# Split-weight slots shifted by 128 bytes each, and odd projection tiles streamed backwards

## The chip, the cores and the metric

The kernel runs on one core of one Trainium2 chip. Its time is the device time of that core in microseconds. It stood at 1546.92 us, the median of two executions (1546.09 and 1547.75 us).

## The reference

Two transformer blocks, one after the other, on 512 tokens of width 1024, all in float32. The first block: a mixer of spatial gating and a gated delta rule, cross-attention to a memory of 256 tokens, a feed-forward of width 4096 with squared relu. The second: a mixer of a causal convolution and sliding-window attention with rotary positions, and a gated feed-forward of width 2816. Nearly all of the arithmetic is in projections, products of the 512 tokens with a weight matrix, between norms:

```
proj = h @ w_in                                  # 1024 x 4104
return jnp.concatenate([y_a, y_b], axis=-1) @ w_out
q = (h @ w_q) ; k = (m @ w_k) ; v = (m @ w_v) ; o @ w_o
return jnp.square(jax.nn.relu(h @ w1)) @ w2      # 1024 x 4096, 4096 x 1024
proj = u @ w_in[l] + b_in[l]                     # 1024 x 5888
up, gate = jnp.split(u @ w_ffn_up[l], 2, axis=-1)
x = x + (jax.nn.silu(a) * gate) @ w_ffn_down[l]
```

## The kernel before

**Layout.** Activations lie transposed: 128 channels on the partitions, the 512 tokens along the free dimension, eight such tiles for the width of 1024. A projection is cut into output tiles of 128 channels. `WEIGHTS` (`weight_order`, line 73) lists 274 of them in the order in which they are multiplied, each as (name, n, k0, k1): output tile n of the matrix called name, over the input tiles k0 to k1, mostly eight.

**Split products.** A float32 product is made of three products in float32r: operands are split into a high part (rounded to float32r by a copy on ScalarE) and a low part (the rest, subtracted on VectorE). For every input tile k, TensorE multiplies high by high, high by low and low by high into the same PSUM bank (lines 1239, 1240 and 1241). The weights are the stationary operand (128x128), the activations the moving one (128x512). So an output tile of eight input tiles is 24 matmuls, each with a load of its own of the stationary operand. The moving operand is in a_hi and a_lo (normed inputs) or b_hi and b_lo (results that are projected again).

**Slots.** Weights come by DMA into w_raw, four slots of 128x1024 (`SLOTS`, 4096 bytes per partition each), tile j in slot j % 4. ScalarE writes w_hi (step `split`, line 1535), VectorE w_lo (step `low`, line 1818), each with four slots too; `split_weights` (line 850) names the place of tile j. The split of tile j waits until tile j - 4 is multiplied. The load into w_raw of tile j waits for both splits of tile j - 4. The eight tiles that come last are kept from an earlier use (`KEPT`), four of them in a_hi and a_lo. The first three tiles are loaded and split together, input tile by input tile (step `front`).

**Order.** `SCHEDULE`, written partly by hand, is one list of steps that all engines go through; each step of an engine waits on semaphores for its operands. Projection steps (`mm`) use banks 0 to 3, tile j bank j % 4; the work between (norms, the delta rule, attention, transposes, all in plain float32) uses banks 4 to 7. Tile j waits until tile j - 4 has been read out of its bank, which VectorE does in most cases.

**Widths.** The moving operand has 512 columns save in the projection of the memory's keys (xa_wk, 256), in the last output tiles (`HALVES`: down2a and down2b, 256 tokens each) and in xa_wv, where the roles are turned (lines 1207 to 1209).

**Places in a partition.** The buffers lie one after the other in the order of their declarations, each start rounded up to 32 bytes. w_raw, w_hi, w_lo, a_hi and a_lo are whole multiples of 512 bytes and begin at the same place of a 512-byte line; line_pad (96 bytes) brings the region of xs, b_hi and b_lo to that place too. Every 128x128 block of the stationary operand is 512 bytes per partition, so it begins at that place as well.

Of the kernel before, what the change touches and what calls it, by code (L numbers as in the profile page):

```python
# [9 lines left out]
F32R = mybir.dt.float32r  # L10
# [5 lines left out]
P = 128  # L16
D = 1024
KT = D // P
S = 512
# [19 lines left out]
SLOTS = 4  # L39
# [4 lines left out]
STRIP = 32  # L44
# [695 lines left out]
def chunk(c):  # L740
    return slice(c * P, (c + 1) * P)


def build_program(nc, x_in, mem_in, front_in, logits_in, weights_in, ws_in, columns_in, rows_in, sinks_in, matrices_in,
                  positions_in, out):
    with ExitStack() as base:
        def sbuf(name, shape, dtype=F32, stack=None):
            return (stack or base).enter_context(nc.sbuf_tensor(name, shape, dtype))
# [9 lines left out]

        raw = sbuf("w_raw", [P, SLOTS, KT * P])
        raw_front = raw[:, 0:FRONT, :].rearrange("p j c -> p (j c)").rearrange("p (t c) -> p t c", t=KT)  # L760
        w_hi = sbuf("w_hi", [P, SLOTS, KT * P], F32R)
        w_lo = sbuf("w_lo", [P, SLOTS, KT * P], F32R)
        a_hi = sbuf("a_hi", [P, KT, S], F32R)
        a_lo = sbuf("a_lo", [P, KT, S], F32R)
        columns = sbuf("columns", [P, N_COLUMNS])
# [83 lines left out]

        def split_weights(j):  # L850
            if j < FIRST_EXTRA:
                return w_hi[:, j % SLOTS, :], w_lo[:, j % SLOTS, :]
            at = (j - FIRST_EXTRA) * 2
            return tuple(a[:, at:at + 2, :].rearrange("p t s -> p (t s)") for a in (a_hi, a_lo))

# [301 lines left out]
        def tensor_program(pe):  # L1157
# [22 lines left out]
            for kind, n in SCHEDULE:  # L1180
# [11 lines left out]
                elif kind == "mm" and WEIGHTS[n[0]][0] == "xa_wv":  # L1192
                    j = n[0]
# [7 lines left out]
                    for i in range(2):  # L1201
                        k, at = first + i, slice(i * S, (i + 1) * S)
                        q.wait_ge(*stage_act.at((A_MEMORY, k)))
                        q.wait_ge(*stage_dve.at((A_MEMORY, k)))
                        for c in range(MC):
                            to = value_bank(half, c)
                            pe.matmul(to, m_hi[:, k, chunk(c)], w_hi[:, j % SLOTS, at], start=k == 0, stop=False)  # L1207
                            pe.matmul(to, m_hi[:, k, chunk(c)], w_lo[:, j % SLOTS, at], start=False, stop=False)  # L1208
                            t = pe.matmul(to, m_lo[:, k, chunk(c)], w_hi[:, j % SLOTS, at], start=False, stop=k == KT - 1)  # L1209
                    t.then_inc(mm_pe.handle, 1)  # L1210
                elif kind == "mm":
                    j, ka, kb = n
                    name, i, k0, k1 = WEIGHTS[j]
                    tokens = HALVES[name][1] if name in HALVES else slice(0, S)
                    width = M if name in ("xa_wk", "xa_wv") else tokens.stop - tokens.start
                    to, loaded = banks[j % BANKS][:, 0:width], j if j < N_LOADS else j - KEPT
                    weights_hi, weights_lo = split_weights(loaded)
# [8 lines left out]
                    for k in range(ka, kb):  # L1226
                        if name in OPERAND:
                            g = OPERAND[name]
                            hi, lo = (m_hi[:, k, :], m_lo[:, k, :]) if g == A_MEMORY else (a_hi[:, k, :], a_lo[:, k, :])
                            q.wait_ge(*stage_act.at((g, k)))  # L1230
                            q.wait_ge(*stage_dve.at((g, k)))
                        else:
                            g = b_generation(name, k0)
                            t = k - k0
                            hi, lo = b_hi[:, b_slot(g, t), tokens], b_lo[:, b_slot(g, t), tokens]
                            q.wait_ge(*b_act.at((g, t)))
                            q.wait_ge(*b_dve.at((g, t)))
                        at = slice((k - k0) * P, (k - k0 + 1) * P)
                        pe.matmul(to, weights_hi[:, at], hi, start=k == k0, stop=False)  # L1239
                        pe.matmul(to, weights_hi[:, at], lo, start=False, stop=False)  # L1240
                        t = pe.matmul(to, weights_lo[:, at], hi, start=False, stop=k == k1 - 1)  # L1241
# [8 lines left out]
                elif kind == "root" and n == A_LAST:  # L1250
                    to = side("sum", n)
# [5 lines left out]
                    for c in range(MC):  # L1257
                        t = pe.matmul(to[:, c:c + 1], square("square", (n, KT - 1))[:, chunk(c)], ones[:, 0:1], start=False, stop=c == MC - 1)
# [11 lines left out]
                elif kind == "row":  # L1270
                    width = M if n in (A_MEMORY, *HALF_OF) else S
# [6 lines left out]
                elif kind == "logits":  # L1278
# [4 lines left out]
                    for k in range(KT // STRIPS):  # L1283
                        for c in range(STRIPS):
                            at = c * (KT // STRIPS) + k
                            t = pe.matmul(side("logits")[strip(c), :], logits_w[:, at, :], x0[:, at, :], start=k == 0, stop=k == KT // STRIPS - 1)
                    t.then_inc(logits_pe.handle, 1)
                elif kind == "rates" and n == 0:
# [4 lines left out]
                    for c in range(NC):  # L1293
                        t = pe.matmul(logits[:, c, :], temp("logits")[:, chunk(c)], half_matrix(SUM_STRIPS)[:, 0:2 * H], start=True, stop=True)
# [12 lines left out]
                elif kind == "sums":  # L1307
# [3 lines left out]
                    for c in range(NC):  # L1311
                        t = pe.transpose(side("sums", n)[:, chunk(c)], qkv[:, n, chunk(c)], eye)
                    t.then_inc(sums_pe.handle, 1)
                elif kind == "statistics":
# [3 lines left out]
                    for c in range(NC):  # L1318
                        t = pe.transpose(bank[:, chunk(c)], temp("v", n)[:, chunk(c)], eye)
                    t.then_inc(statistics_pe.handle, 1)  # L1320
                elif kind == "mix":
# [4 lines left out]
                    for c in range(NC):  # L1326
                        t = pe.matmul(bank[:, chunk(c)], temp("normed", n)[:, chunk(c)], ws[:, n, :], start=True, stop=True)
# [6 lines left out]
                elif kind == "strict":  # L1334
# [6 lines left out]
                    for c in range(NC):  # L1341
                        pe.matmul(kk_bank[:, chunk(c)], kh[:, c, :], kh[:, c, :], start=True, stop=True)
                        t = pe.matmul(qk_bank[:, chunk(c)], kh[:, c, :], qh[:, c, :], start=True, stop=True)
                    t.then_inc(strict_pe.handle, 1)
                elif kind == "turn":
# [3 lines left out]
                    for c in range(NC):  # L1349
                        for part in BLOCKS:  # L1350
                            t = pe.matmul(blocked(bank)[part, c, :], inv_tb[n % 2][part, c, :], half_matrix(EYE_BLOCKS)[part, :],
                                          start=True, stop=True)
                    t.then_inc(turn_pe.handle, 1)
                elif kind == "level_y":
# [10 lines left out]
                    for c in range(NC):  # L1365
                        if level < LEVELS - 1:
                            for part in BLOCKS:
                                t = pe.matmul(blocked(bank)[part, c, :], b[part, c, :], x[part, c, :], start=True, stop=True)  # L1368
                        else:
                            t = pe.matmul(blocked(bank)[BLOCKS[1], c, :], strict_t[h % 2][BLOCKS[0], c, BLOCKS[1]], x[BLOCKS[0], c, :],  # L1370
                                          start=True, stop=True)
# [1090 lines left out]
```

## Time and profile before

| | |
|---|---|
| Two executions | 1546.09 us, 1547.75 us; median 1546.92 us |
| Profiled execution, first to last instruction (span) | 1544.6 us |
| TensorE busy | 1534.5 us, 99% of the span, 8150 matmuls |
| Weight loads busy | 1270.0 us, 82% |
| VectorE, ScalarE, GpSimd busy | 875.9 us (57%), 605.9 us (39%), 103.5 us (7%) |
| Read from HBM | 143.29 MB, 94 GB/s over the span |

The page has no time of the profiled execution beside its span. A busy time is the union of an engine's instructions; matmuls overlap in the records, so the busy times of groups of matmuls add up to more than the span, and the mean duration of one is longer than the distance to the next. The distance between two starts is read from the instructions in order of time. The chain of waits follows the work back from the last instruction. Idle time of VectorE or ScalarE costs nothing as long as TensorE is not waiting for them.

### The profile page before, as it was taken

How to read it: one execution, taken by the hardware profiler on the slowest of the kernel's cores; microseconds unless marked ns; L12 is line 12 of the kernel's file. 1: busy time of each engine (PE TensorE's matmuls, PEld its weight loads, DVE VectorE, ACT ScalarE, POOL GpSimd, SP SyncE). 2: the span in 40 equal slices, each digit the busy share in tenths (PEclk: the TensorE clock that was granted, in tenths of full speed). 3: DMA queues.
4: the chain of work that ended last, by engine and by line, in shares of the span. 5: the costliest groups of instructions: out<-in, count | busy, mean ns of one | idle time of the engine just before them, and what ended most of it. 6: DMA issues, size and time to landing. Idle time of an engine off the chain costs nothing.

```text
span 1544.6 us, 20434 instructions
## 1 busy us (share of the span) xinstructions
PE 1534.5 (99%) x8150; PEld 1270.0 (82%) x8150; DVE 875.9 (57%) x1336; ACT 605.9 (39%) x979; POOL 103.5 (7%) x87
## 2 busy tenths in 40 slices
PE   9999999999999999999999999999999999999998
PEld 7888889887788888888888887877888888888887
DVE  7777766654454343436556777543555653664565
ACT  6546334533343241323556343533244331332333
POOL 0000202110020000000140000100011000000000
PEclk9999999999999999999999999999999999999999
DMA  7121213521133223222322232222332232222212
GB/s 269 56 69 35 77 69 125 189 82 57 57 106 109 94 86 107 95 97 89 108 96 68 84 114 91 94 77 69 116 104 87 99 107 96 92 99 98 93 63 74
DMA packets 44861, 146.70 MB, mean 95 GB/s; under 512 B 4960, under 2 KB 8288, under 8 KB 44640
## 3 DMA queue, kind: packets, MB, share of 16 engines
q1 hardware_dynamic: 42592, 141.93, 27.3%
q10 hardware_dynamic: 2176, 3.47, 0.7%
q8 instruction: 65, 1.06, 0.3%
q14 instruction: 28, 0.23, 0.0%
HBM read 143.29 MB, written 2.10 MB: 94 GB/s over the span
## 4 chain that ended last, share of the span: by engine, by line
PE 98%; issue 1%; DVE 0%; DMA 0%; ACT 0%; POOLq 0%; POOL 0%; DVEq 0%; SPq 0%; ACTq 0%
PE bank L1239 29%; PE bank L1241 29%; PE bank L1240 29%; PE bank L1457 1%; PE bank L1474 1%; PE bank L1368 1%; PE bank L1396 1%; PE bank L1401 1%; PE bank L1491 0%; PE bank L1207 0%; PE bank L1209 0%; PE bank L1208 0%; PE bank L1514 0%; PE bank L1503 0%; PE bank L1169 0%
## 5 line engine op out<-in xcount | busy, mean ns | idle before, releaser
L1239 PE MATMUL bank<-a_hi,w_hi 128*128 128x512 f32 (+1 forms) x1275 | 497.2, 390 | 0.0
L1241 PE MATMUL bank<-a_hi,w_lo 128*128 128x512 f32 (+1 forms) x1275 | 490.0, 384 | 0.0
L1240 PE MATMUL bank<-a_lo,w_hi 128*128 128x512 f32 (+1 forms) x1275 | 489.6, 384 | 0.0
L1818 DVE TENSOR_TENSOR w_lo<-w_raw,w_hi 128x1024 fp32r<-128x1024 f32 (+2 forms) x259 | 327.3, 1268 | 146.6 <-ACT w_hi L1535 146.2
L1535 ACT ACTIVATE w_hi<-w_raw 128x1024 fp32r<-128x1024 f32 (+2 forms) x259 | 266.2, 1034 | 206.8 <-PE bank L1241 198.2
L1239 PEld LDWEIGHTS bank<-a_hi,w_hi 128*128 128x128 f32 x1275 | 239.6, 188 | 49.3 <-issue 2.4
L1241 PEld LDWEIGHTS bank<-a_hi,w_lo 128*128 128x128 f32 x1275 | 239.5, 188 | 48.0
L1240 PEld LDWEIGHTS bank<-a_lo,w_hi 128*128 128x128 f32 x1275 | 239.7, 188 | 45.8 <-issue 0.2
L1239 PE MATMUL bank<-b_hi,w_hi 128*128 128x512 f32 (+1 forms) x720 | 276.5, 384 | 0.0
L1240 PE MATMUL bank<-b_lo,w_hi 128*128 128x512 f32 (+1 forms) x720 | 275.1, 382 | 0.0
L1241 PE MATMUL bank<-b_hi,w_lo 128*128 128x512 f32 (+1 forms) x720 | 275.1, 382 | 0.0
L1239 PEld LDWEIGHTS bank<-b_hi,w_hi 128*128 128x128 f32 x720 | 135.3, 188 | 26.8 <-issue 0.9
L1240 PEld LDWEIGHTS bank<-b_lo,w_hi 128*128 128x128 f32 x720 | 135.4, 188 | 26.3 <-issue 0.2
L1241 PEld LDWEIGHTS bank<-b_hi,w_lo 128*128 128x128 f32 x720 | 135.3, 188 | 26.3
L2102 DVE TENSOR_TENSOR xs<-xs,bank 128x512 f32<-128x512 f32 (+1 forms) x88 | 55.9, 636 | 127.9 <-PE bank L1241 120.8
L1802 DVE TENSOR_TENSOR temp<-bank,rstd 128x512 f32<-128x512 f32 x101 | 69.3, 687 | 64.0 <-PE bank L1241 59.4
L1810 DVE SCALAR_TENSOR_TENSOR temp<-temp,columns 128x512 f32<-128x512 f32 x96 | 72.2, 752 | 28.6 <-ACT temp L1774 17.2
L2290 POOL TENSOR_TENSOR square_sum<-square_sum,square 128x512 f32<-128x512 f32 x28 | 39.8, 1422 | 616.4 <-ACT square L1570 616.4
L2080 DVE TENSOR_TENSOR b_lo<-temp,b_hi 128x512 fp32r<-128x512 f32 x62 | 42.9, 692 | 59.3 <-ACT b_hi L1676 59.0
L1676 ACT ACTIVATE b_hi<-temp 128x512 fp32r<-128x512 f32 x62 | 39.2, 633 | 84.0 <-DVE temp L2259 58.3
L1717 ACT ACTIVATE temp<-temp 128x512 f32<-128x512 f32 x32 | 20.2, 632 | 93.2 <-DVE temp L2155 93.2
L2281 POOL TENSOR_TENSOR narrow<-narrow,columns 128x4 f32<-128x4 f32 (+1 forms) x13 | 19.4, 1494 | 412.1 <-DVE narrow L1861 375.3
(319 smaller groups left out, 1198.3 us busy)
## 6 DMA issues: line engine op xcount, KB each, us to landing
w_raw<-weights_in SPq DMA_DIRECT2D x247, 512.0 KB, 3.2
w_raw<-weights_in SPq DMA_DIRECT2D x8, 384.0 KB, 2.9
x_first<-x_in SPq DMA_DIRECT2D x8, 256.0 KB, 5.9
xs<-x_in ACTq DMA_DIRECT2D x2, 1024.0 KB, 10.8
w_raw<-weights_in SPq DMA_DIRECT2D x8, 256.0 KB, 2.7
mem_x<-mem_in SPq DMA_DIRECT2D x1, 1024.0 KB, 7.8
out<-xs SPq DMA_DIRECT2D x8, 128.0 KB, 1.8
w_raw<-front_in SPq DMA_DIRECT2D x5, 192.0 KB, 5.9
```

What stands on the lines that cost most here:

```text
L1239: pe.matmul(to, weights_hi[:, at], hi, start=k == k0, stop=False)
L1240: pe.matmul(to, weights_hi[:, at], lo, start=False, stop=False)
L1241: t = pe.matmul(to, weights_lo[:, at], hi, start=False, stop=k == k1 - 1)
L1535: act.activation(split_weights(n)[0][:, 0:size], raw[:, n % SLOTS, 0:size], ACT.Copy).then_inc(split_act.handle, 1)
L1676: act.activation(b_hi[:, b_slot(g, i), :], x, ACT.Copy).then_inc(b_act.handle, 1)
L1717: act.activation(temp("relu", n), temp("relu", n), ACT.Square).then_inc(relu_act.handle, 1)
L1802: return dve.tensor_tensor(to, full(name, n, k0)[0:to.shape[0], 0:width], scale[0:to.shape[0], 0:width], ALU.mult)
L1810: dve.scalar_tensor_tensor(acc, buf[:, at:at + S], weight(i), acc, ALU.mult, ALU.add).then_inc(done.handle, 1)
L1818: dve.tensor_tensor(lo[:, 0:size], raw[:, n % SLOTS, 0:size], hi[:, 0:size].bitcast(F32), ALU.subtract).then_inc(split_dve.handle, 1)
L2080: dve.tensor_tensor(lo, x, hi.bitcast(F32), ALU.subtract).then_inc(b_dve.handle, 1)
L2102: dve.tensor_tensor(xs[:, t, tokens], xs[:, t, tokens], full(name, t, k0)[:, 0:tokens.stop - tokens.start], ALU.add).then_inc(residual_dve ...
L2290: pool.tensor_tensor(total, total, square("square", n)[:, 0:total.shape[1]], ALU.add).then_inc(square_pool.handle, 1)
```

## The change

w_hi and w_lo get 32 more elements (`STRIP`, 128 bytes) per slot, which no instruction reads or writes; slot s then begins s x 128 bytes further in a 512-byte line than slot 0. Everything behind the two buffers moves by 2 x 4 x 128 = 1024 bytes. In the projection steps, an output tile with odd n (here i) and a moving operand of 512 columns reads that operand from the last token to the first, and writes its bank from the last column to the first, in all three matmuls of each input tile; the bank then holds what it held before. Tiles with even n, those of 256 columns, xa_wv and the first three tiles (n = 0, 4 and 8 of qkv) run forward.

```diff
--- before.py
+++ after.py
@@ -758,8 +758,8 @@
 
         raw = sbuf("w_raw", [P, SLOTS, KT * P])
         raw_front = raw[:, 0:FRONT, :].rearrange("p j c -> p (j c)").rearrange("p (t c) -> p t c", t=KT)
-        w_hi = sbuf("w_hi", [P, SLOTS, KT * P], F32R)
-        w_lo = sbuf("w_lo", [P, SLOTS, KT * P], F32R)
+        w_hi = sbuf("w_hi", [P, SLOTS, KT * P + STRIP], F32R)
+        w_lo = sbuf("w_lo", [P, SLOTS, KT * P + STRIP], F32R)
         a_hi = sbuf("a_hi", [P, KT, S], F32R)
         a_lo = sbuf("a_lo", [P, KT, S], F32R)
         columns = sbuf("columns", [P, N_COLUMNS])
@@ -849,7 +849,7 @@
 
         def split_weights(j):
             if j < FIRST_EXTRA:
-                return w_hi[:, j % SLOTS, :], w_lo[:, j % SLOTS, :]
+                return w_hi[:, j % SLOTS, 0:KT * P], w_lo[:, j % SLOTS, 0:KT * P]
             at = (j - FIRST_EXTRA) * 2
             return tuple(a[:, at:at + 2, :].rearrange("p t s -> p (t s)") for a in (a_hi, a_lo))
 
@@ -1236,6 +1236,11 @@
                             q.wait_ge(*b_act.at((g, t)))
                             q.wait_ge(*b_dve.at((g, t)))
                         at = slice((k - k0) * P, (k - k0 + 1) * P)
+                        if i % 2 and width == S:
+                            pe.matmul(to[:, ::-1], weights_hi[:, at], hi[:, ::-1], start=k == k0, stop=False)
+                            pe.matmul(to[:, ::-1], weights_hi[:, at], lo[:, ::-1], start=False, stop=False)
+                            t = pe.matmul(to[:, ::-1], weights_lo[:, at], hi[:, ::-1], start=False, stop=k == k1 - 1)
+                            continue
                         pe.matmul(to, weights_hi[:, at], hi, start=k == k0, stop=False)
                         pe.matmul(to, weights_hi[:, at], lo, start=False, stop=False)
                         t = pe.matmul(to, weights_lo[:, at], hi, start=False, stop=k == k1 - 1)
```

## Rows read from the trace of the kernel before

**Rows 1.** The page: span, busy time by engine, granted clock by slice.

```profile
span 1544.6 us, 20434 instructions
...
PE 1534.5 (99%) x8150; PEld 1270.0 (82%) x8150; DVE 875.9 (57%) x1336; ACT 605.9 (39%) x979; POOL 103.5 (7%) x87
...
PEclk9999999999999999999999999999999999999999
```

**Rows 2.** The page: the chain that ended last, by engine and line.

```profile
PE 98%; issue 1%; DVE 0%; DMA 0%; ACT 0%; POOLq 0%; POOL 0%; DVEq 0%; SPq 0%; ACTq 0%
PE bank L1239 29%; PE bank L1241 29%; PE bank L1240 29%; PE bank L1457 1%; PE bank L1474 1%; PE bank L1368 1%; PE bank L1396 1%; PE bank L1401 1%; PE bank L1491 0%; PE bank L1207 0%; PE bank L1209 0%; PE bank L1208 0%; PE bank L1514 0%; PE bank L1503 0%; PE bank L1169 0%
```

**Rows 3.** TensorE's waits: us in total, times, longest us.

```profile
PE bank L1179 <- DVE warm L1785: 1.3, 1, 1.3
PE bank L1169 <- POOL narrow L2281: 1.0, 1, 1.0
PE bank L1185 <- ACT w_hi L1538: 0.7, 1, 0.7
PE bank L1258 <- ACT square L1570: 0.6, 1, 0.6
PE bank L1368 <- DVE inv_tb L2035: 0.5, 1, 0.5
```

**Rows 4.** Matmuls in time, 512 columns: start us, us, what.

```profile
699.69 0.39 PE L1240 MATMUL bank<-b_lo,w_hi 128*128 128x512 f32 x1
...
701.96 0.39 PE L1241 MATMUL bank<-b_hi,w_lo 128*128 128x512 f32 x1
```

**Rows 5.** Matmuls in time, 256 columns, last projections.

```profile
1504.74 0.28 PE L1240 MATMUL bank<-b_lo,w_hi 128*128 128x256 f32 x1
...
1506.42 0.28 PE L1239 MATMUL bank<-b_hi,w_hi 128*128 128x256 f32 x1
```

**Rows 6.** TensorE's groups by shape: xcount, busy us, mean ns.

```profile
L1239 PE MATMUL bank<-a_hi,w_hi 128*128 128x512 f32 x1211 | 478.5, 395 | 0.0
...
L1239 PE MATMUL bank<-b_hi,w_hi 128*128 128x512 f32 x672 | 262.7, 391 | 0.0
```

**Rows 7.** The same view, line 1457 with either half of the keys.

```profile
L1457 PE MATMUL bank<-mem_k_late,xa_q 128*128 128x256 f32 x32 | 7.2, 379 | 0.0
L1457 PE MATMUL bank<-mem_k_early,xa_q 128*128 128x256 f32 x32 | 7.2, 379 | 0.0
```

**Rows 8.** The page: groups of the splits and of b_lo.

```profile
L1818 DVE TENSOR_TENSOR w_lo<-w_raw,w_hi 128x1024 fp32r<-128x1024 f32 (+2 forms) x259 | 327.3, 1268 | 146.6 <-ACT w_hi L1535 146.2
L1535 ACT ACTIVATE w_hi<-w_raw 128x1024 fp32r<-128x1024 f32 (+2 forms) x259 | 266.2, 1034 | 206.8 <-PE bank L1241 198.2
...
L2080 DVE TENSOR_TENSOR b_lo<-temp,b_hi 128x512 fp32r<-128x512 f32 x62 | 42.9, 692 | 59.3 <-ACT b_hi L1676 59.0
```

**Rows 9.** VectorE's split, ns min/median/max, from the view of w_hi.

```profile
L1818 DVE TENSOR_TENSOR w_lo<-w_raw,w_hi x259: 684/1225/2240, 22.3 to 1504.7; 128x1024 fp32r<-128x1024 f32 x120, 128x512 fp32r<-128x512 f32 x8, 128x768 fp32r<-128x768 f32 x2
```

**Rows 10.** VectorE in time in the feed-forward, idle before in brackets.

```profile
561.01 0.69 DVE L2155 SCALAR_TENSOR_TENSOR temp<-bank,rstd 128x512 f32<-128x512 f32 x1 [1.21 <-PE bank L1241]
563.07 0.69 DVE L2080 TENSOR_TENSOR b_lo<-temp,b_hi 128x512 fp32r<-128x512 f32 x1 [1.36 <-ACT b_hi L1676]
564.02 1.23 DVE L1818 TENSOR_TENSOR w_lo<-w_raw,w_hi 128x1024 fp32r<-128x1024 f32 x1 [0.26 <-ACT w_hi L1535]
```

**Rows 11.** Line 1474, plain float32, 512 columns, in time, as a group.

```profile
353.42 3.59 PE L1474 MATMUL bank<-probs_t,mem_v 128*128 128x512 f32 x8
...
L1474 PE MATMUL bank<-probs_t,mem_v 128*128 128x512 f32 x32 | 14.4, 592 | 0.0
```

**Rows 12.** A stream and the weight load beside it, in time.

```profile
700.14 0.39 PE L1239 MATMUL bank<-b_hi,w_hi 128*128 128x512 f32 x1
700.15 0.19 PEld L1240 LDWEIGHTS bank<-b_lo,w_hi 128*128 128x128 f32 x1
```

## The prediction

> **What bounds the kernel now.** I read the engine totals first, then the chain of work that ended last, then the projections' matmuls, grouped and one by one. TensorE is busy for 1534.5 us of a span of 1544.6 us, at a granted clock of 1.0 in nearly every slice, and no other engine is above 57% [rows 1]. The chain is 98% TensorE, and lines 1239 to 1241, the three matmuls of a projection step, hold 87% of it [rows 2]. So a nanosecond on each of these matmuls reaches the end, and one on another engine does not as long as TensorE doesn't wait for it. The waits say how far that holds: its five longest come to 4.1 us in all [rows 3].
>
> What is to be seen in single matmuls is the distance from one start to the next, since the modelled durations (about 390 ns) overlap. In the middle of the kernel eleven 512-column matmuls start from 699.69 to 701.96 us: ten steps of 227 ns [rows 4]. In the last projections fifteen 256-column ones start from 1504.74 to 1506.42: fourteen steps of 120 ns [rows 5]. The difference, 107 ns for 256 columns, is 0.417 ns a column (the 2.4 GHz level of the clock); 512 columns are 213.3 ns, and what remains is 13.3 ns per matmul at either width. Stream and remainder are the two things that the change could touch. It touches many: the 512-column form stands 3 x (1211 + 672) = 5649 times [rows 6], and counting the weight order, 2832 of these belong to tiles with odd number. 5649 x 0.227 = 1282 us, 83% of the span.
>
> **The change, part by part.** No instruction, semaphore, DMA or wait is added, removed or moved. Three properties change.
>
> 1. *The slots' places.* In w_hi and w_lo slots 1, 2 and 3 move on by 128, 256 and 384 bytes, and everything after them by 1024 bytes, two whole 512-byte lines, so no other operand changes its place in a line. For TensorE the stationary operand of three slots in four now starts elsewhere in a line than the moving operand; so far both start at the same place. The trace has this difference once: at line 1457 the stationary operand is xa_q and the moving one mem_k_early for half of the heads, mem_k_late for the other half. From the declarations mem_k_early (4096 bytes), warm (1032, rounded up to 1056) and line_pad (96) fill 5248 bytes ahead of the region of xs, ten lines and 128 bytes; mem_k_late lies whole lines behind it, as xa_q does. So the early half stands 128 bytes off and the late half doesn't. Both took 7.2 us for 32 matmuls, mean 379 ns [rows 7]. That is plain float32, the nearest row that there is. I take 0 ns. Bounds: were the full remainder a price of coinciding places, it would go in three slots of four, 4644 matmuls by the weight order, 13.3 ns each: -62 us. The other way, that the shift costs, I bound by half of that remainder again on the same matmuls, +31 us; the pair at line 1457 speaks against both.
>    The Trainium skill (TensorE: Matmul & The Clock Gate, Step-by-step: what each phase is for) says that TensorE reads the moving operand and the weights through two independent ports, so that loading weights takes nothing from a running matmul. The pair at line 1457 agrees; by that rule the shift gives 0.
>
> 2. *The splits that write the slots.* ScalarE writes w_hi (1034 ns mean, 259 times), VectorE w_lo (1268 ns) [rows 8]. A write that starts 128 bytes on could change their pace. The nearest row is b_lo from temp (692 ns at 512 elements): it reads five temp buffers of 2060 bytes, which begin at five different places of a line, against 684 ns for the shortest of the splits, in which all operands begin alike [rows 8, 9]. I take nothing. What hides a change is that ScalarE's splits wait 198.2 us in all for TensorE to free a slot [rows 8], up to three tiles (24 x 227 ns = 5.4 us each) before the result is read. In a tile of the feed-forward VectorE is busy 0.69 + 0.69 + 1.23 = 2.6 us of 5.4 [rows 10]. Even splits half as long again (+0.6 us a tile) fit. If the cover were gone each tile would pay at most that: 0.6 x 259 = 155 us, which needs VectorE full, and it is at 57%.
>
> 3. *Backward streams.* 2832 matmuls read their 512 tokens from last to first and write their bank from last to first. The banks hold the same values in the same places, a tile is backward in all its 24 matmuls, and its reader waits for the last, so nothing waits longer or shorter. The price is in the stream alone, and the trace shows no operand that descends. From below: a gain of the remainder, 2832 x 13.3 ns = -38 us. From above: if either side takes one column where it takes two now, the 213.3 ns of a stream double: 2832 x 213.3 ns = +604 us. I take 0, the nearer row being the ascending form itself: every element that a backward stream touches lies beside the one before it, as in the forward one, and the start at token 511 is the end of a line that is used whole.
>    The Trainium skill (SBUF — State Buffer, Door 1: The DMA port swizzle) states that SBUF is read in lines of 16 bytes, at full rate when a line is hit at least twice in succession, and that PSUM has lines of 8 bytes, with any non-contiguous PSUM pattern slowing matmuls significantly. A backward float32 stream hits a 16-byte line four times and an 8-byte line twice, so counting hits it gives 0; counting a step of -1 as non-contiguous it gives the slow rival below. No row of this trace decides between the two.
>
> The sum: 0 + 0 + 0 on the span of 1544.6 us. The two executions took 1546.09 and 1547.75 us, 1.5 and 3.2 us above that span, median 1546.92; I forecast 1547.
>
> **The rivals.**
>
> *A. Slower: backward streams run at half rate.* Place: the three matmuls of the new branch. Price per backward matmul 213.3 ns, start to start 440 ns; 1547 + 604 = 2151 us, with nothing to hide it, since TensorE is the chain. It decides (over 2%) from 31 us / 2832 = 11 ns per matmul. For it: at 0.417 ns a column two neighbours may well travel together, and pairing may be built for ascending addresses. The trace shows that streams can be handled differently by kind: the plain float32 matmuls of 512 columns start 429 ns apart ((3.59 - 0.59) / 7) [rows 11], two streams of 213.3 ns and 2 ns, without the 13.3. Against it: nothing here but the contiguity. Chance 0.17.
>
> *B. A little slower: a fixed cost of starting backward, or of changing direction.* As large as the remainder again on each backward matmul: +38 us, 1585 us. A cost on the change of direction alone (at most 137 odd tiles, two changes each) stays under 4 us even at 13.3 ns and would not be noticed. Chance of more than 2%: 0.04.
>
> *C. Faster: part of the 13.3 ns is a clash of the weight load with the stream in the same place of a line.* For it: the load of the next weights starts within 0.01 us of the stream before it and runs beside it for 0.19 us, both from the start of a line [rows 12]. Without the remainder on slots 1 to 3: 1547 - 62 = 1485 us; on the backward tiles alone 1509 us. Against it: the remainder is the same 13.3 ns with half of the columns, ten steps in a row over all three lines keep the same 227 ns [rows 4], where a clash should scatter; and the pair at line 1457 differs by nothing. Chance 0.07.
>
> *D. The change does nothing on the chip*, because a stream reversed on both sides is issued forward: 1547 us as well. It is in the forecast's case, and only the weight slots would then be tried.
>
> **How the numbers follow.** A measurement of this kernel can tell about 2% from no change, 31 us here. Within 2%: 0.72 (the forecast with D, and small costs under B). Slower: A 0.17 + B 0.04 = 0.21. Faster: C 0.07. The forecast's own range is 1540 to 1556. The range starts there and takes in C down to its larger bound, 1485, and B up to 1588 (38 us and the 3 us by which executions lie over the span); that holds 0.83. A, at 2151, is left out.
>
> **What the profile after would show.** Right: start-to-start steps of 227 ns on the three new lines as on the old three, x672 and x1211 divided about in half among them, TensorE still 98% of the chain, splits within a few ns of 1034 and 1268. Rival A: 440 ns on the new lines and 227 on the old ones, and VectorE's share falling to about 40% for the same work. Rival B: 228 to 241 ns on the new lines. Rival C: under 227 ns on slots 1 to 3, with slot 0 left at 227, or on the new lines alone. The forecast is wrong if the step of either kind moves by more than 11 ns on half of the matmuls.

## The result and the profile after

The changed kernel takes 1576.72 us (1576.41 and 1577.02) against 1546.92 us: ratio 1.0193, 95% interval 1.0163 to 1.0223, 29.8 us slower. The interval has 2% in it, so whether the change stays within 2% isn't decided. The prediction said 1547 us with a range of 1485 to 1588.

The page after, in the lines that answer to [rows 1, 2 and 8]: span and busy times, granted clock, the chain, the splits.

```profile
span 1575.3 us, 20434 instructions
...
PE 1564.7 (99%) x8150; PEld 1271.5 (81%) x8150; DVE 877.2 (56%) x1336; ACT 605.8 (38%) x979; POOL 103.3 (7%) x87
...
PEclk9999999999999999999999999999999999999999
...
PE 98%; issue 1%; DMA 0%; DVE 0%; ACT 0%; SPq 0%; POOLq 0%; POOL 0%; DVEq 0%
PE bank L1244 15%; PE bank L1246 15%; PE bank L1245 15%; PE bank L1240 14%; PE bank L1241 14%; PE bank L1242 14%; PE bank L1462 1%; PE bank L1479 1%; PE bank L1373 1%; PE bank L1401 1%; PE bank L1406 1%; PE bank L1496 0%; PE bank L1209 0%; PE bank L1207 0%; PE bank L1208 0%
...
L1823 DVE TENSOR_TENSOR w_lo<-w_raw,w_hi 128x1024 fp32r<-128x1024 f32 (+2 forms) x259 | 327.2, 1267 | 147.4 <-ACT w_hi L1540 147.0
L1540 ACT ACTIVATE w_hi<-w_raw 128x1024 fp32r<-128x1024 f32 (+2 forms) x259 | 266.0, 1034 | 215.5 <-PE bank L1246 107.7
```

The span grew by 30.7 us and TensorE's busy time by 30.2 us. Instruction counts, the clock in tenths and the shares of the chain are the same, and the splits take 1267 and 1034 ns as before (1268 and 1034). So the time went into the matmuls themselves. Lines 1239 to 1241 of before are now 1240 to 1242 in backward tiles and 1244 to 1246 in forward ones.

What shows it is the time from one start to the next. From here on one spot serves for all kernels: output tiles 4, 5, 6 and 7 of ffn_w2 in the third part of the first feed-forward, which lie in slots 0, 1, 2 and 3. Of each tile two rows stand, the first matmul of its input tile 3 and the last matmul of its input tile 7, fourteen steps later (start us, duration us, then what it is). Starts are rounded to 0.01 us, so that a mean step from them is good to 0.7 ns; the same spot in the kernel before has 226 or 227 ns in all four. After, in slots 0 and 1:

```profile
694.81 0.39 PE L1244 MATMUL bank<-b_hi,w_hi 128*128 128x512 f32 x1
...
697.98 0.40 PE L1246 MATMUL bank<-b_hi,w_lo 128*128 128x512 f32 x1
...
700.34 0.40 PE L1240 MATMUL bank<-b_hi,w_hi 128*128 128x512 f32 x1
...
703.65 0.40 PE L1242 MATMUL bank<-b_hi,w_lo 128*128 128x512 f32 x1
```

Tile 4, forward in slot 0: 3.17 us / 14 = 226.4 ns, as before [rows 4]. Tile 5, backward in slot 1: 3.31 / 14 = 236.4 ns. Over the whole trace the start-to-start times of neighbouring 512-column matmuls (5574 pairs), sorted by slot and kind of tile, come to these means. The slots are even or odd, "odd tile" is one with odd n, backward where the kernel has backward tiles:

| mean step, ns | before | shift only | backward only | after |
|---|---|---|---|---|
| even slot, even tile (2146) | 228.2 | 228.9 | 228.9 | 229.6 |
| odd slot, even tile (637) | 230.1 | 235.3 | 230.1 | 235.4 |
| even slot, odd tile (681) | 229.3 | 229.9 | 235.4 | 235.4 |
| odd slot, odd tile (2110) | 228.1 | 234.0 | 234.6 | 236.8 |

(The means before lie above 226.7 because pairs with a stall between them are in. A pair counts for the tile of its first matmul.) The middle columns are the first two experiments.

### The profile page after: what moved, and what is told of

The parts are those of the page before. It is cut to its first block, busy times and chain, and to the rows that moved or that the text cites. A ratio compares the mean times of both kernels' runs of the same rounds, so it can differ in the third digit from the quotient of the medians.

```text
span 1575.3 us, 20434 instructions
## 1 busy us (share of the span) xinstructions
PE 1564.7 (99%) x8150; PEld 1271.5 (81%) x8150; DVE 877.2 (56%) x1336; ACT 605.8 (38%) x979; POOL 103.3 (7%) x87
## 4 chain that ended last, share of the span: by engine, by line
PE 98%; issue 1%; DMA 0%; DVE 0%; ACT 0%; SPq 0%; POOLq 0%; POOL 0%; DVEq 0%
PE bank L1244 15%; PE bank L1246 15%; PE bank L1245 15%; PE bank L1240 14%; PE bank L1241 14%; PE bank L1242 14%; PE bank L1462 1%; PE bank L1479 1%; PE bank L1373 1%; PE bank L1401 1%; PE bank L1406 1%; PE bank L1496 0%; PE bank L1209 0%; PE bank L1207 0%; PE bank L1208 0%
## 5 line engine op out<-in xcount | busy, mean ns | idle before, releaser
L1823 DVE TENSOR_TENSOR w_lo<-w_raw,w_hi 128x1024 fp32r<-128x1024 f32 (+2 forms) x259 | 327.2, 1267 | 147.4 <-ACT w_hi L1540 147.0
L1540 ACT ACTIVATE w_hi<-w_raw 128x1024 fp32r<-128x1024 f32 (+2 forms) x259 | 266.0, 1034 | 215.5 <-PE bank L1246 107.7
L1244 PE MATMUL bank<-a_hi,w_hi 128*128 128x512 f32 (+1 forms) x667 | 258.0, 387 | 0.0
L1246 PE MATMUL bank<-a_hi,w_lo 128*128 128x512 f32 (+1 forms) x667 | 254.6, 382 | 0.0
L1245 PE MATMUL bank<-a_lo,w_hi 128*128 128x512 f32 (+1 forms) x667 | 254.2, 381 | 0.0
L1240 PE MATMUL bank<-a_hi,w_hi 128*128 128x512 f32 x608 | 245.2, 403 | 0.0
L1241 PE MATMUL bank<-a_lo,w_hi 128*128 128x512 f32 x608 | 242.0, 398 | 0.0
L1242 PE MATMUL bank<-a_hi,w_lo 128*128 128x512 f32 x608 | 241.9, 398 | 0.0
L1244 PE MATMUL bank<-b_hi,w_hi 128*128 128x512 f32 (+1 forms) x384 | 145.6, 379 | 0.0
L1240 PE MATMUL bank<-b_hi,w_hi 128*128 128x512 f32 x336 | 134.6, 400 | 0.0
L1242 PE MATMUL bank<-b_hi,w_lo 128*128 128x512 f32 x336 | 134.1, 399 | 0.0
L1241 PE MATMUL bank<-b_lo,w_hi 128*128 128x512 f32 x336 | 134.1, 399 | 0.0
```

What stands on the lines that cost most here:

```text
L1240: pe.matmul(to[:, ::-1], weights_hi[:, at], hi[:, ::-1], start=k == k0, stop=False)
L1241: pe.matmul(to[:, ::-1], weights_hi[:, at], lo[:, ::-1], start=False, stop=False)
L1242: t = pe.matmul(to[:, ::-1], weights_lo[:, at], hi[:, ::-1], start=False, stop=k == k1 - 1)
L1540: act.activation(split_weights(n)[0][:, 0:size], raw[:, n % SLOTS, 0:size], ACT.Copy).then_inc(split_act.handle, 1)
L1823: dve.tensor_tensor(lo[:, 0:size], raw[:, n % SLOTS, 0:size], hi[:, 0:size].bitcast(F32), ALU.subtract).then_inc(split_dve.handle, 1)
```

## The experiments

Two theories came from this table's last column. *Place*: a stationary operand that begins off the moving one costs. *Direction*: a backward stream costs. The *distance* of the two operands is how many bytes further on in a line the stationary one begins. "Steps" below are means over input tiles 3 to 7 of all tiles away from other work, unless two rows are named.

**The parts alone.** Shift only, against the changed kernel (the branch of the backward tiles goes):

```diff
-                        if i % 2 and width == S:
-                            ...
-                            continue
```

> The shift of the slots alone, all tiles forward. Place theory (a stationary operand that begins 128 or 384 bytes off the moving one costs about 5.6 ns a matmul, one that begins 0 or 256 bytes off costs nothing, as the steps of the changed kernel's forward tiles read): slots 1 and 3 go to about 232 to 233 ns a step, slots 0 and 2 stay at 227, about 2800 x 5.6 ns = +16 us, 1563 us. Direction theory (only the backward streams cost): 227 ns in all slots, 1547 us.

Measured: 1565.37 us (4 runs), ratio 1.0120 (1.0103 to 1.0137), +18.5 us. The same two tiles as above, slots 0 and 1:

```profile
690.12 0.39 PE L1239 MATMUL bank<-b_hi,w_hi 128*128 128x512 f32 x1
...
693.29 0.40 PE L1241 MATMUL bank<-b_hi,w_lo 128*128 128x512 f32 x1
...
695.63 0.39 PE L1239 MATMUL bank<-b_hi,w_hi 128*128 128x512 f32 x1
...
698.88 0.40 PE L1241 MATMUL bank<-b_hi,w_lo 128*128 128x512 f32 x1
```

3.17 / 14 = 226 ns and 3.25 / 14 = 232 ns. Over the trace: 226.7, 232.4, 226.7 and 232.4 ns in slots 0 to 3. Distances of 128 and 384 bytes cost 5.7 ns a matmul, 256 bytes nothing. The first matmuls of a tile behind a shifted one pay too (232 and 231 ns against 227 for the second and third step), and the first step inside a shifted tile takes 241; that is most of what lies between the forecast 16 and the measured 18.5 us.

Backward only, slots as before, against the changed kernel (the slices in `split_weights` go back too):

```diff
-        w_hi = sbuf("w_hi", [P, SLOTS, KT * P + STRIP], F32R)
-        w_lo = sbuf("w_lo", [P, SLOTS, KT * P + STRIP], F32R)
+        w_hi = sbuf("w_hi", [P, SLOTS, KT * P], F32R)
+        w_lo = sbuf("w_lo", [P, SLOTS, KT * P], F32R)
```

> The backward streams alone, slots unshifted. Direction theory: 233.3 ns a step in every backward tile, 227 in every forward one, 2832 x 6.6 ns = +19 us, 1566 us. Place theory (the backward streams cost only because a shifted slot meets them): 227 ns everywhere, 1547 us. A cost of the change of direction alone would show in the first steps of a tile and leave the rest at 227: under 4 us.

Measured: 1566.47 us (4 runs), ratio 1.0128 (1.0112 to 1.0143), +19.6 us. Slots 0 (forward) and 1 (backward):

```profile
690.45 0.39 PE L1244 MATMUL bank<-b_hi,w_hi 128*128 128x512 f32 x1
...
693.62 0.39 PE L1246 MATMUL bank<-b_hi,w_lo 128*128 128x512 f32 x1
...
695.95 0.40 PE L1240 MATMUL bank<-b_hi,w_hi 128*128 128x512 f32 x1
...
699.22 0.40 PE L1242 MATMUL bank<-b_hi,w_lo 128*128 128x512 f32 x1
```

3.17 / 14 = 226 ns and 3.27 / 14 = 234 ns; over the trace 233.3 ns in every backward tile and 226.7 in every forward one. Both theories hold, each for its part. A change of direction costs a little besides (238 and 232 ns in the first two steps of a forward tile behind a backward one, against 227).

**Backward everywhere.** The same branch with the condition `j >= FRONT and width == S`.

> All tiles of 512 columns backward but the first three, slots unshifted: no change of direction from tile to tile. If the cost is of the backward stream itself: 233.3 ns everywhere, 5586 x 6.6 ns = +37 us, 1584 us. If it is a matter of mixing directions: near 227 ns, 1547 us.

Measured: 1582.02 us (one run), 233.3 ns in all slots; slot 0:

```profile
695.47 0.40 PE L1240 MATMUL bank<-b_hi,w_hi 128*128 128x512 f32 x1
...
698.73 0.40 PE L1242 MATMUL bank<-b_hi,w_lo 128*128 128x512 f32 x1
```

3.26 / 14 = 233 ns. The cost is of the backward stream, 6.7 ns each, not of mixing directions. All backward matmuls have 512 columns, so whether it is a fixed cost or grows with the columns isn't shown.

**Everything moved by 128 bytes.**

```diff
+        sbuf("lead_pad", [P, STRIP])
         raw = sbuf("w_raw", [P, SLOTS, KT * P])
```

> 128 unused bytes ahead of all buffers, all forward: every operand begins 128 bytes further in its line, none moves against another. If only the distance between stationary and moving operand counts: 227 ns a step, 1547 us. If the place of the stationary operand in the line itself counts (the changed kernel's slot 1 stood there): about 232 ns in every slot, 5649 x 5.6 ns = +32 us, 1579 us.

Measured: 1546.49 us (one run), 226.7 ns in all slots; slot 1:

```profile
688.25 0.39 PE L1240 MATMUL bank<-b_hi,w_hi 128*128 128x512 f32 x1
...
691.42 0.39 PE L1242 MATMUL bank<-b_hi,w_lo 128*128 128x512 f32 x1
```

The stationary operands of all slots stand where slot 1 stood in the changed kernel, and nothing is lost, since the moving operands went along. What counts is the distance between the two.

**Reading or writing backwards.** First only the moving operand backwards, then only the bank, in odd tiles, against the run with backward tiles only (the other two matmuls alike):

```diff
-                            pe.matmul(to[:, ::-1], weights_hi[:, at], hi[:, ::-1], start=k == k0, stop=False)
+                            pe.matmul(to, weights_hi[:, at], hi[:, ::-1], start=k == k0, stop=False)
```

```diff
-                            pe.matmul(to[:, ::-1], weights_hi[:, at], hi[:, ::-1], start=k == k0, stop=False)
+                            pe.matmul(to[:, ::-1], weights_hi[:, at], hi, start=k == k0, stop=False)
```

> In the odd tiles only the moving operand is read backwards, the bank is written forwards, so their 512 tokens land in reversed order (the kernel computes something else there). Slots unshifted. If the cost of a backward stream lies in reading: 233.3 ns a step in the odd tiles, as with reading and writing backwards, 1566 us. If it lies in writing: 227 ns, 1547 us. If each side costs on its own and they overlap: near 233 here and in the next run too.

> In the odd tiles only the bank is written backwards, the moving operand is read forwards (tokens reversed again). If the cost lies in writing: 233.3 ns a step in the odd tiles, 1566 us. If in reading: 227 ns, 1547 us.

Measured: 1567.03 us reading backwards, 1546.87 us writing backwards (one run each). Slot 1, an odd tile, in the first and in the second:

```profile
696.48 0.40 PE L1240 MATMUL bank<-b_hi,w_hi 128*128 128x512 f32 x1
...
699.75 0.40 PE L1242 MATMUL bank<-b_hi,w_lo 128*128 128x512 f32 x1
```

```profile
688.27 0.39 PE L1240 MATMUL bank<-b_hi,w_hi 128*128 128x512 f32 x1
...
691.44 0.39 PE L1242 MATMUL bank<-b_hi,w_lo 128*128 128x512 f32 x1
```

3.27 / 14 = 234 ns against 3.17 / 14 = 226 ns. The whole 6.7 ns lie in the reading; writing the bank backwards cost nothing here.

**How the distance counts.** First all slots off by the same 128 bytes:

```diff
+        sbuf("slot_pad", [P, STRIP])
         w_hi = sbuf("w_hi", [P, SLOTS, KT * P], F32R)
         w_lo = sbuf("w_lo", [P, SLOTS, KT * P], F32R)
+        sbuf("back_pad", [P, 3 * STRIP])
```

> All slots of w_hi and w_lo begin 128 bytes off the moving operands, alike, all tiles forward. Place theory, distance between stationary and moving operand: every slot behaves as slots 1 and 3 do in the run with the shift alone, mean step 232.4 ns, 5600 x 5.7 ns = +32 us, 1579 us. Rival, the cost comes from slots that differ among each other (the weight loads of neighbouring tiles): 227 ns, 1547 us.

Measured: 1580.29 us (one run), 233.0 to 233.2 ns in all slots (expected 232.4); slot 0:

```profile
695.10 0.39 PE L1241 MATMUL bank<-b_hi,w_hi 128*128 128x512 f32 x1
...
698.36 0.39 PE L1243 MATMUL bank<-b_hi,w_lo 128*128 128x512 f32 x1
```

So slots need not differ among each other. Why 128 bytes cost 0.7 ns more here than in the run with the shift alone isn't known. Then steps of 32 bytes from slot to slot, with pads behind w_hi and w_lo that keep the rest in its place of a line (`split_weights` takes the first 1024 elements of a slot, as in the change):

```diff
+        w_hi = sbuf("w_hi", [P, SLOTS, KT * P + 8], F32R)
+        sbuf("mid_pad", [P, 96])
+        w_lo = sbuf("w_lo", [P, SLOTS, KT * P + 8], F32R)
+        sbuf("back_pad", [P, 96])
```

> Slots begin 0, 32, 64 and 96 bytes off the moving operand, all tiles forward; the rest stays in place. If only the distance modulo 256 bytes in halves counts (off 128: dear, within a half: free): 227 ns in all slots, 1547 us. If any distance costs in proportion: steps that grow from slot 1 to slot 3 up to 232 ns, 1555 us. If a distance of 32, 64 or 96 bytes avoids part of the 13 ns that a matmul takes beyond its stream: below 227 ns in slots 1 to 3, a way to a faster kernel.

Measured: 1574.69 us (one run). Slots 0 to 3:

```profile
692.95 0.39 PE L1241 MATMUL bank<-b_hi,w_hi 128*128 128x512 f32 x1
...
696.12 0.40 PE L1243 MATMUL bank<-b_hi,w_lo 128*128 128x512 f32 x1
...
698.45 0.40 PE L1241 MATMUL bank<-b_hi,w_hi 128*128 128x512 f32 x1
...
701.72 0.39 PE L1243 MATMUL bank<-b_hi,w_lo 128*128 128x512 f32 x1
...
704.05 0.39 PE L1241 MATMUL bank<-b_hi,w_hi 128*128 128x512 f32 x1
...
707.32 0.39 PE L1243 MATMUL bank<-b_hi,w_lo 128*128 128x512 f32 x1
...
709.65 0.39 PE L1241 MATMUL bank<-b_hi,w_hi 128*128 128x512 f32 x1
...
712.93 0.39 PE L1243 MATMUL bank<-b_hi,w_lo 128*128 128x512 f32 x1
```

226, 234, 234 and 234 ns; over the trace 226.7, 233.3, 233.4 and 234.3. All three expectations miss for 512 columns: neither is a half of 256 bytes one place, nor does the price grow much with the distance, nor does one help. The same with 2 elements a slot instead of 8 (pads of 120):

> Slots begin 0, 8, 16 and 24 bytes off the moving operand, all forward: how fine the places count. If any distance off 0 modulo 256 bytes costs 6 to 7 ns: about 233 ns in slots 1 to 3, 1575 us. If places within 32 bytes are one place: 226.7 ns everywhere, 1547 us. If a small distance helps: below 226.7 ns.

Measured: 1565.78 us (one run), 226.7, 230.8, 233.0 and 230.2 ns in slots 0 to 3. All three miss again: 8 bytes already cost, but 8 and 24 cost less than 16. And to the other side, by slots laid out in reverse order behind a pad:

```diff
+        sbuf("slot_pad", [P, 40])
+        w_hi = sbuf("w_hi", [P, SLOTS, KT * P + 8], F32R)[:, ::-1, :]
+        sbuf("mid_pad", [P, 32])
+        w_lo = sbuf("w_lo", [P, SLOTS, KT * P + 8], F32R)[:, ::-1, :]
+        sbuf("back_pad", [P, 56])
```

> Slots 3, 2, 1 and 0 begin 160, 192, 224 and 256 bytes past the moving operand's place (in 256-byte terms 96, 64, 32 and 0 bytes short of it), all forward. If the distance modulo 256 bytes counts and is the same in both directions: 234.3, 233.3, 233.3 and 226.7 ns a step in slots 3 to 0, 1575 us. If slots that lag are free and slots that lead cost (or one of them meets less of the stream than distance 0 does): steps of 226.7 ns or below in slots 1 to 3, 1547 us or less.

Measured: 1569.07 us (one run). Slots 1, 2 and 3:

```profile
696.52 0.40 PE L1242 MATMUL bank<-b_hi,w_hi 128*128 128x512 f32 x1
...
699.79 0.39 PE L1244 MATMUL bank<-b_hi,w_lo 128*128 128x512 f32 x1
...
702.07 0.39 PE L1242 MATMUL bank<-b_hi,w_hi 128*128 128x512 f32 x1
...
705.28 0.40 PE L1244 MATMUL bank<-b_hi,w_lo 128*128 128x512 f32 x1
...
707.62 0.39 PE L1242 MATMUL bank<-b_hi,w_hi 128*128 128x512 f32 x1
...
710.89 0.39 PE L1244 MATMUL bank<-b_hi,w_lo 128*128 128x512 f32 x1
```

233, 229 and 234 ns; over the trace 233.2, 229.2 and 233.5. The distances of the expectation hold for w_lo alone: from the declarations slots 1, 2 and 3 of w_lo begin 224, 192 and 160 bytes past the moving operand's place, and those of w_hi 32, 64 and 96 bytes short of it. Modulo 256 bytes the two are the same, and only so are they named below. The price isn't the same in both directions: 192 costs 2.5 ns where 64 costs 6.7. Of eleven distances modulo 256 bytes only 0 costs nothing, the others 2.5 to 7.6 ns, and none is faster than 0. A version that beats the kernel before didn't come out of this.

**The same slots with 256 columns.** Each of these runs also holds float32r matmuls with 256 columns, in xa_wk and in the last output tiles, whose slots moved along. No expectation was about them. Of xa_wk, first matmul of input tile 3 and last of input tile 7: output tile 1 before, output tile 1 in the run with steps of 8 bytes (8 bytes off), output tile 2 in the run with steps of 32 (64 bytes off):

```profile
217.90 0.28 PE L1239 MATMUL bank<-a_hi,w_hi 128*128 128x256 f32 x1
...
219.58 0.28 PE L1241 MATMUL bank<-a_hi,w_lo 128*128 128x256 f32 x1
```

```profile
219.44 0.28 PE L1241 MATMUL bank<-a_hi,w_hi 128*128 128x256 f32 x1
...
221.06 0.28 PE L1243 MATMUL bank<-a_hi,w_lo 128*128 128x256 f32 x1
```

```profile
225.77 0.28 PE L1241 MATMUL bank<-a_hi,w_hi 128*128 128x256 f32 x1
...
227.35 0.28 PE L1243 MATMUL bank<-a_hi,w_lo 128*128 128x256 f32 x1
```

1.68 / 14 = 120 ns, 1.62 / 14 = 116 ns and 1.58 / 14 = 113 ns. Over the forward runs, steps inside a tile without those that hold a wait, the means are 119.7 ns at distance 0, 115.9 at 8 bytes, 116.5 at 64, 118.8 at 128, and 116.9 to 120.0 at the others. So with 256 columns no distance is dearer by more than 0.3 ns, and most are up to 4 ns cheaper. The price of a distance belongs to the form with 512 columns; why the width turns its sign isn't known.

**How much load.** Stationary blocks of 64 columns instead of 128, save in the first and the last matmul of a tile; slots unshifted, odd tiles backward:

```diff
+                        half = slice(0, HALF if width == S and j >= FRONT else P)
...
+                            pe.matmul(to[half, ::-1], weights_hi[:, at][:, half], lo[:, ::-1], start=False, stop=False)
...
+                        pe.matmul(to[half, :], weights_hi[:, at][:, half], lo, start=False, stop=False)
```

> Slots unshifted, odd tiles backward. All 512-column matmuls but the first and the last of each tile load 64 columns of the stationary operand instead of 128 and write 64 partitions: half of the projections' outputs are left incomplete. Theory: what goes beyond the stream of 213.3 ns is lost while the weight load and the moving stream read at the same time, so half as much load costs half as much: about 220 ns forward (13.3 / 2), 223 ns backward (20 / 2), 1510 us. Rival: 13.3 ns and the 6.7 ns of a backward read are fixed costs of a matmul: 226.7 and 233.3 ns as before, 1566 us. If only the backward part hangs on the load: 226.7 and 230 ns.

Measured: 1572.56 us (one run). The load of one line as a group (count, busy us, mean ns, idle before), and slots 0 (forward) and 1 (backward):

```profile
L1248 PEld LDWEIGHTS bank<-a_lo,w_hi 128*64 128x64 f32 x600 | 80.6, 134 | 52.1 <-issue 0.2
```

```profile
691.40 0.40 PE L1247 MATMUL bank<-b_hi,w_hi 128*64 128x512 f32 x1
...
694.62 0.39 PE L1249 MATMUL bank<-b_hi,w_lo 128*128 128x512 f32 x1
...
696.95 0.40 PE L1243 MATMUL bank<-b_hi,w_hi 128*64 128x512 f32 x1
...
700.22 0.40 PE L1245 MATMUL bank<-b_hi,w_lo 128*128 128x512 f32 x1
```

The load takes 134 ns instead of 188, and the steps don't fall: 230 ns forward (226.7 with the full load), 234 backward (233.3). My theory, that the time beyond the stream is lost in proportion to the load beside it, fell; so did its variant for the backward part. The rival gave the backward step rightly and the forward one too low. Forward matmuls became 3.5 ns dearer. The run halves what is loaded and the partitions that are written, so which of the two does that isn't shown.

**Backward at other distances.** The slots of 32-byte steps with the branch of the run with all tiles backward:

> All 512-column tiles but the first three backward, slots 0, 32, 64 and 96 bytes off the moving operand. If the 6.7 ns of a backward read are fixed and a distance adds its price as in forward streams: 233.3 ns in slot 0, about 240 in slots 1 to 3, 1605 us. If a backward read is dear because its walk meets the weight load's at the wrong places: another distance suits it, and slot 1, 2 or 3 falls below 233.3 ns, towards 226.7. If the two costs cover each other: 233 to 236 ns in all slots, 1585 to 1595 us.

Measured: 1581.47 us (one run), 233.3 ns in all four slots; slots 1 and 3:

```profile
700.78 0.40 PE L1242 MATMUL bank<-b_hi,w_hi 128*128 128x512 f32 x1
...
704.05 0.40 PE L1244 MATMUL bank<-b_hi,w_lo 128*128 128x512 f32 x1
...
711.98 0.40 PE L1242 MATMUL bank<-b_hi,w_hi 128*128 128x512 f32 x1
...
715.25 0.40 PE L1244 MATMUL bank<-b_hi,w_lo 128*128 128x512 f32 x1
```

3.27 / 14 = 234 ns in both. The same distances that cost 6.6 to 7.6 ns forward cost nothing on top of a backward read in the mean: the two cover each other, as the third expectation had it, down to 233.3, and 3.5 us below its time. In the changed kernel, with 128 and 384 bytes, backward steps are 235.4 and 236.4 ns, so there the cover isn't whole.

## Why the prediction was right or wrong

The range held the time, but the forecast's own range of 1540 to 1556 didn't: two of its three terms were wrong. The range held because its upper end was a rival's, 38 us for backward streams, and not by the forecast's mechanism. The measured 1.93% lies under 2%, with an interval that reaches past it, and that is luck too: the two parts together cost 8.2 us less than their sum, which would have been 2.5%.

**The reading of the bound held.** TensorE is still 98% of the chain, and a few nanoseconds on each of some thousand matmuls came out at the end: 29.8 us. The steps named as what to look at showed the cost at once.

**Part 1, the slots' places: failed.** Taken as 0 from the pair at line 1457 [rows 7], measured +18.5 us alone, inside the bound of +31. The price fell on the 2787 matmuls with 512 columns in slots 1 and 3, 5.7 ns each or 15.9 us, and on first steps of tiles. The pair was the wrong row to lean on, for two reasons that it doesn't separate. It is plain float32, whose matmuls take two streams of their length and 2 ns beside them [rows 11], where the projections' take one and 13.3 ns. And it has 256 columns, with which the shifted float32r matmuls didn't get dearer either (118.8 ns at 128 bytes against 119.7). No row of before had a shifted operand with 512 columns. The forecast's quotation of the Trainium skill (TensorE: Matmul & The Clock Gate, Step-by-step: what each phase is for), that the two read ports keep a weight load from taking anything from a running matmul, doesn't give the right number for these matmuls: the distance of the two operands alone moves the step from 226.7 to as much as 234.3 ns. No run took the load away, so whether it is the load that takes this from the stream isn't shown.

**Part 2, the splits: held.** 1267 and 1034 ns, and ScalarE sat idle before its splits for 215.5 us against 206.8 [rows 8].

**Part 3, backward streams: failed in its value.** Taken as 0, measured +19.6 us alone, 2832 x 6.7 ns = 19.0 us, and the changes of direction for the rest. Contiguity, my reason, didn't settle the reading side. Of the two readings that I gave of the Trainium skill (SBUF — State Buffer, Door 1: The DMA port swizzle), counting hits per line holds on the bank's side (0 ns) and not on SBUF's (6.7 ns with four hits a line), and the slow rival's doubling, 213.3 ns, is out by a factor of 32.

**The rivals.** B, a cost on each backward matmul, is what part 3 did, at half of its assumed price (that it is fixed isn't shown); it had a chance of 0.04 as a case beyond 2%, and the shift, which it didn't count, added as much again. That makes +29.8 us, just under the 31 us where it would have been "slower". A and C didn't happen. What C looked at, whether the operands begin in the same place of a line, does matter, with the sign turned for 512 columns: there the same place is the cheap one. Its clash was ruled out among other things because ten steps keep the same 227 ns; at 128 bytes single steps do scatter, from 228 to 241 ns in the run with the shift alone, where at distance 0 nearly all are 226 or 227. With 256 columns the sign is C's, up to 4 ns of the 13.3, on too few matmuls to show in the time. D is out: backward streams took 233.3 ns a step, and forward ones 226.7.

**The sum.** Alone the parts cost 18.5 and 19.6 us, 38.0 together before rounding, and both at once 29.8. The table has the missing 8.2 us: three in four backward tiles lie in odd slots (2110 of 2791 pairs), and there, before rounding, the shift alone adds 5.8 ns and the direction alone 6.5, but both 8.6 and not 12.3. The 3.7 ns that don't add up, on 2136 such matmuls, are 7.9 us.

**What stays open.** Why the distance matters, and why only with 512 columns. The price lies between two operands that are both read, and doesn't grow steadily with the distance. Forward, 0 and 256 bytes cost the same and so do 128 and 384, but on backward streams 128 and 384 differ by 1 ns. No slot was shifted in the run with half the load, so what a distance costs beside a smaller load isn't known. A stationary operand read backwards was not tried, nor a backward stream of another width, nor was the 13.3 ns at distance 0 taken apart.

## What to carry to other kernels

In a kernel that TensorE bounds, write down what each matmul takes from start to start beyond its stream, and look at where both operands begin: here, with 512 columns, stationary and moving operand in the same place modulo 256 bytes took 226.7 ns and every other placement tried 229 to 234, up to 33.5 us in all. With 256 columns no placement was dearer, so try it at the width that the kernel has. If a stream must be turned round, turn it on the bank's side, which cost nothing here, and not in the reading. Before a cost is taken as zero from a neighbouring row, ask whether that row is the same form of instruction, in type and in width; and a bound of a few nanoseconds times 5649 deserves a price of its own rather than a zero.

## What the hardware showed that I had not expected

- Steps of float32r matmuls with 512 columns by the distance of the stationary from the moving operand, forward (160, 192 and 224 modulo 256): 0 and 256 bytes 226.7 ns; 8: 230.8; 16: 233.0; 24: 230.2; 32: 233.3; 64: 233.4; 96: 234.3; 128 and 384: 232.4 (233.1 with all slots there); 160: 233.5; 192: 229.2; 224: 233.2.
- The same with 256 columns: 119.7 ns at 0, 115.9 at 8 bytes, 116.5 at 64, 118.8 at 128, and none above 120.0.
- A moving operand read backwards, 512 columns: 233.3 ns at distances of 0, 32, 64, 96 and 256 bytes, 235.4 and 236.4 at 128 and 384. A bank written backwards: 226.7 ns.
- A stationary block of 64 columns, with 64 partitions written, made forward steps longer, 230.2 ns, though its load was 54 ns shorter.
